# Order of the products inside a weight slot: feed-forward slots by length, projection slots by half of the weights

## The chip, the cores and the metric

The kernel runs on one core of a Trainium2 chip. Time is the device time of one execution in microseconds (us), median over several executions; lower is better.

## The reference, cut to what matters

The input is one sequence of 256 tokens of width 1024, in f32. A first block of two layers comes first, each with a gated feed-forward of width 2816, a mixer and a second feed-forward; behind it come an "even" layer (stick-breaking attention and a state-space mixer) and an "odd" layer (gated linear attention).

```
h = h + 0.5 * swiglu(rmsnorm(h, ffn1_norm[l]), gate, up, down)      # (silu(x@gate) * (x@up)) @ down
z = rmsnorm(h, mix_norm[l]) @ w_in[l]                               # 5664 columns, split over three branches
h = h + merged @ w_out[l]
h = h + 0.5 * swiglu(rmsnorm(h, ffn2_norm[l]), ...)
...                                                                 # even layer, odd layer: rms_norm(x) @ w_in, mix, @ w_out
```

Most of the arithmetic is products of a 256-row activation with f32 weight matrices, some 260 MB of them in all.

## The kernel before, in words

**Exact products from halves.** TensorE takes 32-bit operands in the type fp32r, which keeps fewer bits than f32. So each operand is split: high = value rounded to fp32r, low = value minus high. A product is high*high + high*low + low*high, all added up in PSUM. `exact3` issues those three as matmuls of 256 columns. For the feed-forward (`wide`, and the down products in `FfnApart.tensor`) the high and the low half of the activation lie side by side, so that one matmul of 512 columns does w_high*(x_high, x_low), and one of 256 columns does w_low*x_high. A reduction on VectorE (`take_wide`) adds the two halves of the bank when it is read.

**Slots.** Weights come in slots of 128 x 2048 (1 MB). Three buffers form a ring. Of each slot n SyncE issues the DMA into `w_raw` (`load`), ScalarE rounds it to `w_high` (`split_high`, L194, counts semaphore hi_made), VectorE subtracts for `w_low` (`split_low`, L201, counts lo_made), and TensorE uses both. `load` of slot n waits for lo_made of slot n-3; `split_high` of slot n waits until TensorE is through with slot n-3 (semaphore bank_filled). Each engine's order is written out by hand in the methods `scalar`, `vector` and `tensor` of each stage.

**What a slot is on TensorE.** A `wide` slot has 8 tiles k of 128 input channels and two groups i of 128 output features: 16 pairs of a 512-column and a 256-column product (L264 and L266), taking turns. There are 88 such slots, 22 in each of four feed-forwards. A down slot of `FfnApart` has 8 tiles, again 16 pairs (L725, L727); there are 33. A `project` slot has 8 tiles, two groups and three products of 256 columns each (L211, L212, L213), 48 products. There are 76: 22 in each of the two mixers, 20 in the even layer, 12 in the odd layer. Other slots (attention latents, branch and output matrices, the down slots of the last feed-forward) call `exact3` by themselves.

**Waits inside a slot.** At the start of a slot TensorE waits for lo_made. The first slot behind a norm also waits, at k = 0, 2, 4 and 6, for the low half of the activation `x` of these two tiles (`norm.x_low`, written at L302 on VectorE; the tiles 6 and 7 come from the last quarter of the stage before: TensorE fills the bank, VectorE reduces it (L242) and adds it to the residual (L691), ScalarE rounds it (L291), VectorE subtracts (L302)). The very first slot of the kernel comes in five pieces (FIRST_TILES: tiles 0; 1; 2, 3; 4, 5; 6, 7), each with its own waits. The argument `midway` calls a few small products in the middle of a slot: the norm's mean (L325, in the first feed-forward L366), latent sums, or transposes. Behind the mean come a square root on ScalarE (L334), a reciprocal on VectorE (L339) and the scaling of what was read from PSUM (L669, L675). VectorE reads a gate slot's banks at L242; the next gate slot waits for that read.

Of the kernel before, what the change touches and what calls it, by code (L numbers as in the profile page):

```python
# [15 lines left out]
P = 128  # L16
SEQ = 256
# [197 lines left out]

def project(c, pe, bank, n, kt, norm=None, tokens=False, width=FC, x=None, midway=None):

    wh, wl = c.weights_at(n, kt, width)
    xh, xl = x or (c.xh, c.xl)
    pe.wait_ge(c.lo_made, c.made(n))  # L220
    for k in range(kt):
        if midway and k == kt // 2:
            midway()
        if norm and k % 2 == 0:
            pe.wait_ge(*norm.x_low(k // 2 + 1))
        for i in range(2):
            start = k == 0 and i == 0
            if tokens:
                t = slice(i * P, (i + 1) * P)
                mm = exact3(pe, c.halves(bank)[:, i, 0:width], xh[:, k, t], xl[:, k, t], wh[:, k, :], wl[:, k, :],  # L230
                            start, k == kt - 1)
            else:
                f = slice(i * P, (i + 1) * P)
                mm = exact3(pe, c.halves(bank)[:, i, :], wh[:, k, f], wl[:, k, f], xh[:, k, :], xl[:, k, :],
                            start, k == kt - 1)
    return mm


# [6 lines left out]
def wide(c, pe, bank, n, norm=None, midway=None):  # L245


    wh, wl = c.weights_at(n, DT, FC)
    if n > 1:
        pe.wait_ge(c.lo_made, c.made(n))  # L250
    for k in range(DT):
        if midway and k == DT // 2:
            midway()
        if norm and n and k % 2 == 0:
            pe.wait_ge(*norm.x_low(k // 2 + 1))
        for b, (first, _) in enumerate(FIRST_TILES if n == 0 else ()):
            if k == first:
                pe.wait_ge(c.xl_made, b + 1)
                pe.wait_ge(c.lo_made, b + 1)
        if n == 1 and k % 4 == 0:  # L260
            pe.wait_ge(c.lo_made, PIECES + 1 + k // 4)
        for i in range(2):
            f = slice(i * P, (i + 1) * P)
            pe.matmul(c.bank(bank + i).rearrange("p (a t) -> p a t", a=2), wh[:, k, f], c.x[:, :, k, :], start=(k == 0),  # L264
                      stop=False, skip_group_check=True)
            mm = pe.matmul(c.bank(bank + i, SEQ), wl[:, k, f], c.xh[:, k, :], start=False, stop=(k == DT - 1),  # L266
                           skip_group_check=True)
    return mm


# [338 lines left out]
class FfnApart(Ffn):  # L609
# [90 lines left out]
    def tensor(self, pe):  # L700
# [12 lines left out]
        for m in range(FF_STEPS):  # L713
            n = base + 2 * FF_STEPS + m
            wh, wl = c.weights_at(n, SLOT_TILES, FC)
            pe.wait_ge(c.lo_made, c.made(n))
            for j in range(SLOT_TILES):
                p, k = divmod(SLOT_TILES * m + j, FF_TILES)
                if p == 0 and k % 2 == 0:
                    pe.wait_ge(*self.hid_low(k // 2 + 1))  # L720
                if p >= 2 and k == 0:
                    pe.wait_ge(*self.down_read(p - 1))
                for i in range(2):
                    f, bank = slice(i * P, (i + 1) * P), B_DOWN + 2 * (p % 2) + i
                    pe.matmul(c.bank(bank).rearrange("p (a t) -> p a t", a=2), wh[:, j, f], b.hid[:, :, k, :], start=(k == 0),  # L725
                              stop=False, skip_group_check=True)
                    mm = pe.matmul(c.bank(bank, SEQ), wl[:, j, f], b.hid[:, 0, k, :], start=False, stop=(k == FF_TILES - 1),  # L727
                                   skip_group_check=True)
                if k == FF_TILES - 1 and m < LAST:
                    mm.then_inc(c.done, 1)  # L730
            mm.then_inc(c.done, 1)

# [2343 lines left out]
```

## Time and profile before

| what | value |
|---|---|
| time, median of 3 runs | 1510.16 us (1507.58 to 1510.79) |
| the profiled execution's own time | 1510.64 us |
| its span | 1508.8 us |
| TensorE (PE) busy | 1499.7 us, 99%, 10908 matmuls |
| weight loads (PEld) busy | 1388.6 us, 92% |
| VectorE (DVE) busy | 1182.3 us, 78% |
| ScalarE (ACT) busy | 792.6 us, 53% |
| mean granted TensorE clock | 0.998 |
| DMA | 261.30 MB, 173 GB/s |

The span runs from the first to the last instruction; 1.8 us of the execution's time lie around it. A matmul in the trace has a start and a modelled end; matmuls overlap, so the "busy" time of one (0.28 us for 256 columns, 0.39 us for 512) is more than the distance to the next. How fast TensorE goes is read from start to start.

### The profile page before, as it was taken

How to read it: one execution, taken by the hardware profiler on the slowest of the kernel's cores; microseconds unless marked ns; L12 is line 12 of the kernel's file. 1: busy time of each engine (PE TensorE's matmuls, PEld its weight loads, DVE VectorE, ACT ScalarE, POOL GpSimd, SP SyncE). 2: the span in 40 equal slices, each digit the busy share in tenths (PEclk: the TensorE clock that was granted, in tenths of full speed). 3: DMA queues.
4: the chain of work that ended last, by engine and by line, in shares of the span. 5: the costliest groups of instructions: out<-in, count | busy, mean ns of one | idle time of the engine just before them, and what ended most of it. 6: DMA issues, size and time to landing. Idle time of an engine off the chain costs nothing.

```text
span 1508.8 us, 25562 instructions
## 1 busy us (share of the span) xinstructions
PE 1499.7 (99%) x10908; PEld 1388.6 (92%) x10908; DVE 1182.3 (78%) x1560; ACT 792.6 (53%) x1003; POOL 39.4 (3%) x41
## 2 busy tenths in 40 slices
PE   8999999999999999999999999999999999999999
PEld 7888899999988888888889999999999999999989
DVE  7987776797888865988758688889998899766744
ACT  6444455565544443544445556455545745775654
POOL 0000001210000000000001020000000000000000
PEclk9999999999999999999999999999999999999999
DMA  7555545434555545555554444465554453325531
GB/s 283 196 196 195 175 167 184 153 140 150 186 185 187 190 173 200 191 180 185 191 191 149 174 151 157 143 227 194 197 194 172 164 193 131 125 106 189 182 126 56
DMA packets 38976, 261.30 MB, mean 173 GB/s; under 512 B 4688, under 2 KB 5584, under 8 KB 9168
## 3 DMA queue, kind: packets, MB, share of 16 engines
q1 hardware_dynamic: 38000, 258.62, 47.8%
q8 instruction: 86, 1.41, 0.4%
q10 hardware_dynamic: 864, 1.05, 0.2%
q14 instruction: 26, 0.21, 0.0%
HBM read 258.61 MB, written 1.05 MB: 172 GB/s over the span
## 4 chain that ended last, share of the span: by engine, by line
PE 94%; DVE 4%; ACT 1%; DMA 0%; issue 0%; ACTq 0%
PE ps L264 22%; PE ps L211 14%; PE ps L213 14%; PE ps L212 14%; PE ps L266 11%; PE ps L725 8%; PE ps L727 4%; DVE w_low L201 2%; PE ps L1448 1%; DMA w_raw<-in_weights 0%; PE ps L1439 0%; PE ps L1421 0%; ACT w_high L194 0%; DVE scratch L2119 0%; PE ps L1463 0%; PE ps L2264 0%
## 5 line engine op out<-in xcount | busy, mean ns | idle before, releaser
L194 ACT ACTIVATE w_high<-w_raw 128x2048 fp32r<-128x2048 f32 (+2 forms) x244 | 459.8, 1886 | 423.2 <-PE ps L266 188.1
L201 DVE TENSOR_TENSOR w_low<-w_raw,w_high 128x2048 fp32r<-128x2048 f32 (+2 forms) x244 | 552.8, 2267 | 127.3 <-ACT w_high L194 125.3
L264 PE MATMUL ps<-x,w_high 128*128 128x512 f32 x1408 | 498.4, 399 | 2.5 <-DVE w_low L878 2.5
L266 PE MATMUL ps<-x,w_low 128*128 128x256 f32 x1408 | 394.8, 280 | 0.0
L264 PEld LDWEIGHTS ps<-x,w_high 128*128 128x128 f32 x1408 | 265.2, 188 | 67.2 <-DVE x L817 2.8
L266 PEld LDWEIGHTS ps<-x,w_low 128*128 128x128 f32 x1408 | 266.3, 189 | 0.1
L211 PE MATMUL ps<-x,w_high 128*128 128x256 f32 x904 | 261.0, 289 | 0.2 <-DVE x L302 0.2
L213 PE MATMUL ps<-x,w_low 128*128 128x256 f32 x904 | 255.7, 283 | 0.0
L212 PE MATMUL ps<-x,w_high 128*128 128x256 f32 x904 | 255.6, 283 | 0.0
L725 PE MATMUL ps<-ffn_hid,w_high 128*128 128x512 f32 x528 | 183.2, 390 | 0.0
L211 PEld LDWEIGHTS ps<-x,w_high 128*128 128x128 f32 x904 | 173.1, 192 | 5.1 <-issue 3.9
L212 PEld LDWEIGHTS ps<-x,w_high 128*128 128x128 f32 x904 | 173.3, 192 | 0.7 <-issue 0.5
L213 PEld LDWEIGHTS ps<-x,w_low 128*128 128x128 f32 x904 | 173.2, 192 | 0.0
L727 PE MATMUL ps<-ffn_hid,w_low 128*128 128x256 f32 x528 | 148.9, 282 | 0.0
L725 PEld LDWEIGHTS ps<-ffn_hid,w_high 128*128 128x128 f32 x528 | 99.1, 188 | 20.8
L727 PEld LDWEIGHTS ps<-ffn_hid,w_low 128*128 128x128 f32 x528 | 99.8, 189 | 0.0
L211 PE MATMUL ps<-w_high,x 128*128 128x256 f32 x320 | 92.3, 289 | 0.0
L213 PE MATMUL ps<-w_high,x 128*128 128x256 f32 x320 | 90.5, 283 | 0.0
L212 PE MATMUL ps<-w_low,x 128*128 128x256 f32 x320 | 90.5, 283 | 0.0
L242 DVE TENSOR_REDUCE ffn_up<-ps 128x512 f32<-128x1024 f32 x44 | 53.8, 1223 | 35.7 <-PE ps L266 35.5
L242 DVE TENSOR_REDUCE ffn_gate<-ps 128x512 f32<-128x1024 f32 x56 | 68.5, 1222 | 10.8 <-PE ps L266 5.1
L211 PE MATMUL ps<-mix_y_high,w_high 128*128 128x256 f32 x224 | 63.6, 284 | 0.0
(456 smaller groups left out, 2359.4 us busy)
## 6 DMA issues: line engine op xcount, KB each, us to landing
w_raw<-in_weights SPq DMA_DIRECT2D x231, 1024.0 KB, 4.8
w_raw<-in_weights SPq DMA_DIRECT2D x10, 768.0 KB, 4.2
w_raw<-in_weights SPq DMA_DIRECT2D x5, 512.0 KB, 3.8
even_second_vectors<-in_second SPq DMA_DIRECT2D x1, 1836.0 KB, 7.2
resid<-in_x SPq DMA_DIRECT2D x3, 256.0 KB, 6.5
w_raw<-in_weights ACTq DMA_DIRECT2D x3, 256.0 KB, 8.0
out<-resid SPq DMA_DIRECT2D x3, 256.0 KB, 2.4
table<-in_table SPq DMA_DIRECT2D x1, 737.0 KB, 8.3
```

Source lines behind the costliest of these rows:

```text
L194: act.activation(self.wh[:, j, 0:SIZES[n]], self.raw[:, j, 0:SIZES[n]], ACT.Copy).then_inc(self.hi_made, 1)
L201: dve.tensor_tensor(self.wl[:, j, 0:SIZES[n]], self.raw[:, j, 0:SIZES[n]], self.wh[:, j, 0:SIZES[n]].bitcast(F32), ALU.subtract).then_inc( ...
L211: pe.matmul(out, ah, bh, start=start, stop=False, skip_group_check=True)
L212: pe.matmul(out, ah, bl, start=False, stop=False, skip_group_check=True)
L213: return pe.matmul(out, al, bh, start=False, stop=stop, skip_group_check=True)
L242: return dve.tensor_reduce(out, c.ps[:, bank:bank + 2, :].rearrange("p f (a t) -> p f t a", a=2), AX.X, ALU.add)
L264: pe.matmul(c.bank(bank + i).rearrange("p (a t) -> p a t", a=2), wh[:, k, f], c.x[:, :, k, :], start=(k == 0), stop=False, skip_group_chec ...
L266: mm = pe.matmul(c.bank(bank + i, SEQ), wl[:, k, f], c.xh[:, k, :], start=False, stop=(k == DT - 1), skip_group_check=True)
L725: pe.matmul(c.bank(bank).rearrange("p (a t) -> p a t", a=2), wh[:, j, f], b.hid[:, :, k, :], start=(k == 0), stop=False, skip_group_check= ...
L727: mm = pe.matmul(c.bank(bank, SEQ), wl[:, j, f], b.hid[:, 0, k, :], start=False, stop=(k == FF_TILES - 1), skip_group_check=True)
L1448: mm = pe.transpose(c.bank(B_T)[:, i * P:(i + 1) * P], m.pr[:, 0, i * P:(i + 1) * P], ident)
```

## The change

In a `wide` slot and in a down slot of `FfnApart` all 512-column products come first and then all 256-column ones. In a down slot that holds the end of one pair of output groups and the start of the next, this is done for each pair by itself. In a `project` slot the products w_high*x_high and w_high*x_low of all tiles come first, then all w_low*x_high. TensorE waits for hi_made ahead of the first part and for lo_made ahead of the second. `midway` is called in the second part of a `wide` slot (still at k = 4), and at k = 6 instead of k = 4 in the first part of a `project` slot. Number, shape and operands of the products are the same, and so are the waits for `x_low`, at the same k. `exact3` and its other callers stay as they are.

```diff
--- before.py
+++ after.py
@@ -215,24 +215,30 @@
 
 def project(c, pe, bank, n, kt, norm=None, tokens=False, width=FC, x=None, midway=None):
 
+
     wh, wl = c.weights_at(n, kt, width)
     xh, xl = x or (c.xh, c.xl)
-    pe.wait_ge(c.lo_made, c.made(n))
+    pe.wait_ge(c.hi_made, c.made(n))
+
+    def product(k, i, w, moved, start=False, stop=False):
+        if tokens:
+            return pe.matmul(c.halves(bank)[:, i, 0:width], moved[:, k, i * P:(i + 1) * P], w[:, k, :], start=start, stop=stop,
+                             skip_group_check=True)
+        return pe.matmul(c.halves(bank)[:, i, :], w[:, k, i * P:(i + 1) * P], moved[:, k, :], start=start, stop=stop,
+                         skip_group_check=True)
+
     for k in range(kt):
-        if midway and k == kt // 2:
+        if midway and k == 3 * kt // 4:
             midway()
         if norm and k % 2 == 0:
             pe.wait_ge(*norm.x_low(k // 2 + 1))
         for i in range(2):
-            start = k == 0 and i == 0
-            if tokens:
-                t = slice(i * P, (i + 1) * P)
-                mm = exact3(pe, c.halves(bank)[:, i, 0:width], xh[:, k, t], xl[:, k, t], wh[:, k, :], wl[:, k, :],
-                            start, k == kt - 1)
-            else:
-                f = slice(i * P, (i + 1) * P)
-                mm = exact3(pe, c.halves(bank)[:, i, :], wh[:, k, f], wl[:, k, f], xh[:, k, :], xl[:, k, :],
-                            start, k == kt - 1)
+            product(k, i, wh, xh, start=k == 0 and i == 0)
+            product(k, i, wh, xl)
+    pe.wait_ge(c.lo_made, c.made(n))
+    for k in range(kt):
+        for i in range(2):
+            mm = product(k, i, wl, xh, stop=k == kt - 1)
     return mm
 
 
@@ -246,25 +252,33 @@
 
 
     wh, wl = c.weights_at(n, DT, FC)
-    if n > 1:
-        pe.wait_ge(c.lo_made, c.made(n))
-    for k in range(DT):
-        if midway and k == DT // 2:
-            midway()
-        if norm and n and k % 2 == 0:
-            pe.wait_ge(*norm.x_low(k // 2 + 1))
+    both = [(k, i, slice(i * P, (i + 1) * P)) for k in range(DT) for i in range(2)]
+
+    def arrived(parts, k):
+        if n > 1 and k == 0:
+            pe.wait_ge(parts, c.made(n))
         for b, (first, _) in enumerate(FIRST_TILES if n == 0 else ()):
             if k == first:
-                pe.wait_ge(c.xl_made, b + 1)
-                pe.wait_ge(c.lo_made, b + 1)
+                pe.wait_ge(parts, b + 1)
         if n == 1 and k % 4 == 0:
-            pe.wait_ge(c.lo_made, PIECES + 1 + k // 4)
-        for i in range(2):
-            f = slice(i * P, (i + 1) * P)
-            pe.matmul(c.bank(bank + i).rearrange("p (a t) -> p a t", a=2), wh[:, k, f], c.x[:, :, k, :], start=(k == 0),
-                      stop=False, skip_group_check=True)
-            mm = pe.matmul(c.bank(bank + i, SEQ), wl[:, k, f], c.xh[:, k, :], start=False, stop=(k == DT - 1),
-                           skip_group_check=True)
+            pe.wait_ge(parts, PIECES + 1 + k // 4)
+
+    for k, i, f in both:
+        if i == 0:
+            if norm and n and k % 2 == 0:
+                pe.wait_ge(*norm.x_low(k // 2 + 1))
+            for b, (first, _) in enumerate(FIRST_TILES if n == 0 else ()):
+                if k == first:
+                    pe.wait_ge(c.xl_made, b + 1)
+            arrived(c.hi_made, k)
+        pe.matmul(c.bank(bank + i).rearrange("p (a t) -> p a t", a=2), wh[:, k, f], c.x[:, :, k, :], start=(k == 0), stop=False,
+                  skip_group_check=True)
+    for k, i, f in both:
+        if i == 0:
+            if midway and k == DT // 2:
+                midway()
+            arrived(c.lo_made, k)
+        mm = pe.matmul(c.bank(bank + i, SEQ), wl[:, k, f], c.xh[:, k, :], start=False, stop=(k == DT - 1), skip_group_check=True)
     return mm
 
 
@@ -713,20 +727,23 @@
         for m in range(FF_STEPS):
             n = base + 2 * FF_STEPS + m
             wh, wl = c.weights_at(n, SLOT_TILES, FC)
-            pe.wait_ge(c.lo_made, c.made(n))
-            for j in range(SLOT_TILES):
-                p, k = divmod(SLOT_TILES * m + j, FF_TILES)
-                if p == 0 and k % 2 == 0:
-                    pe.wait_ge(*self.hid_low(k // 2 + 1))
-                if p >= 2 and k == 0:
-                    pe.wait_ge(*self.down_read(p - 1))
-                for i in range(2):
-                    f, bank = slice(i * P, (i + 1) * P), B_DOWN + 2 * (p % 2) + i
-                    pe.matmul(c.bank(bank).rearrange("p (a t) -> p a t", a=2), wh[:, j, f], b.hid[:, :, k, :], start=(k == 0),
+            pe.wait_ge(c.hi_made, c.made(n))
+            tiles = [(j, *divmod(SLOT_TILES * m + j, FF_TILES)) for j in range(SLOT_TILES)]
+            for pair in sorted({p for _, p, _ in tiles}):
+                own = [(j, k, i, slice(i * P, (i + 1) * P)) for j, p, k in tiles if p == pair for i in range(2)]
+                first = B_DOWN + 2 * (pair % 2)
+                for j, k, i, f in own:
+                    if pair == 0 and i == 0 and k % 2 == 0:
+                        pe.wait_ge(*self.hid_low(k // 2 + 1))
+                    if pair >= 2 and i == 0 and k == 0:
+                        pe.wait_ge(*self.down_read(pair - 1))
+                    pe.matmul(c.bank(first + i).rearrange("p (a t) -> p a t", a=2), wh[:, j, f], b.hid[:, :, k, :], start=(k == 0),
                               stop=False, skip_group_check=True)
-                    mm = pe.matmul(c.bank(bank, SEQ), wl[:, j, f], b.hid[:, 0, k, :], start=False, stop=(k == FF_TILES - 1),
-                                   skip_group_check=True)
-                if k == FF_TILES - 1 and m < LAST:
+                pe.wait_ge(c.lo_made, c.made(n))
+                for j, k, i, f in own:
+                    mm = pe.matmul(c.bank(first + i, SEQ), wl[:, j, f], b.hid[:, 0, k, :], start=False,
+                                   stop=(k == FF_TILES - 1), skip_group_check=True)
+                if own[-1][1] == FF_TILES - 1 and m < LAST:
                     mm.then_inc(c.done, 1)
             mm.then_inc(c.done, 1)
```

## Rows read from the trace of the kernel before

**Rows 1.** Waits of TensorE: who <- whom: us in total, times, longest.

```profile
PE ps L264 <- DVE w_low L878: 2.5, 1, 2.5
...
PE ps L2278 <- DVE scratch L2124: 1.0, 1, 1.0
```

**Rows 2.** Timeline, PE: start us, us, instruction; first products of `wide` and down slots.

```profile
36.08 0.39 PE L264 MATMUL ps<-x,w_high 128*128 128x512 f32 x1
...
130.37 0.39 PE L264 MATMUL ps<-x,w_high 128*128 128x512 f32 x1
...
141.48 0.39 PE L725 MATMUL ps<-ffn_hid,w_high 128*128 128x512 f32 x1
...
191.40 0.39 PE L725 MATMUL ps<-ffn_hid,w_high 128*128 128x512 f32 x1
...
434.45 0.40 PE L264 MATMUL ps<-x,w_high 128*128 128x512 f32 x1
...
536.21 0.40 PE L264 MATMUL ps<-x,w_high 128*128 128x512 f32 x1
```

**Rows 3.** Timeline, PE: six 512-column products in a row, and what follows.

```profile
228.25 0.39 PE L211 MATMUL ps<-w_high,mix_y_high 128*128 128x512 f32 x1
...
229.63 0.28 PE L211 MATMUL ps<-x,w_high 128*128 128x256 f32 x1
```

**Rows 4.** Timeline, PE: runs of 256-column products, first and last start.

```profile
1413.75 0.28 PE L211 MATMUL ps<-x,w_high 128*128 128x256 f32 x1
...
1425.27 0.28 PE L211 MATMUL ps<-w_high,x 128*128 128x256 f32 x1
...
1482.80 0.28 PE L211 MATMUL ps<-odd_o_high,w_high 128*128 128x256 f32 x1
...
1499.70 0.28 PE L211 MATMUL ps<-odd_o_high,w_high 128*128 128x256 f32 x1
```

**Rows 5.** Timeline, PE and DVE: start of slots behind a norm, and x_low.

```profile
196.95 0.28 PE L211 MATMUL ps<-x,w_high 128*128 128x256 f32 x1
...
200.07 0.88 DVE L302 SCALAR_TENSOR_TENSOR x<-resid,vectors,x 128x256 fp32r<-128x256 f32 x2 [0.98 <-ACT x L291]
...
417.06 0.39 PE L264 MATMUL ps<-x,w_high 128*128 128x512 f32 x1
...
418.93 0.88 DVE L302 SCALAR_TENSOR_TENSOR x<-resid,vectors,x 128x256 fp32r<-128x256 f32 x2 [0.98 <-ACT x L291]
...
602.87 0.39 PE L264 MATMUL ps<-x,w_high 128*128 128x512 f32 x1
...
606.00 0.88 DVE L302 SCALAR_TENSOR_TENSOR x<-resid,vectors,x 128x256 fp32r<-128x256 f32 x2 [0.98 <-ACT x L291]
```

**Rows 6.** Timeline, PE and DVE, of the kernel's first slot.

```profile
11.07 0.68 DVE L878 TENSOR_TENSOR w_low<-w_raw,w_high 128x512 fp32r<-128x512 f32 x1
11.67 0.87 DVE L817 SCALAR_TENSOR_TENSOR x<-resid,vectors,x 128x256 fp32r<-128x256 f32 x2
...
11.90 0.47 PE L264 MATMUL ps<-x,w_high 128*128 128x512 f32 x1 [2.51 <-DVE w_low L878]
...
15.29 0.63 PE L264 MATMUL ps<-x,w_high 128*128 128x512 f32 x1
15.71 0.41 PE L266 MATMUL ps<-x,w_low 128*128 128x256 f32 x1
...
17.71 0.39 PE L264 MATMUL ps<-x,w_high 128*128 128x512 f32 x1
```

**Rows 7.** Two stretches: busy us (instructions) of each engine, PEclk, DMA share, GB/s.

```profile
12.59:16.00 3.41, 3.41 (x13) 2.93 (x12) 3.02 (x5) 3.41 (x6) 0.00 (x0) 0.50 0.69 243
...
1252.00:1256.00 4.00, 2.98 (x28) 2.69 (x30) 3.90 (x10) 0.00 (x0) 0.00 (x0) 1.00 0.39 160
```

**Rows 8.** Timeline: the first norm's mean on PE, the second gate read on DVE.

```profile
26.03 1.89 PE L366 MATMUL ps<-scratch,ones 128*128 128x256 f32 x8
...
33.65 1.22 DVE L242 TENSOR_REDUCE ffn_gate<-ps 128x512 f32<-128x1024 f32 x1
```

## The prediction

> **What bounds the kernel now.** I read the page's busy times first: TensorE is busy for 99% of the span, VectorE for 78%, DMA moves 173 GB/s without anyone waiting long for it. The chain of waits says the same, since 94% of it is TensorE. The next view is the waits of TensorE, because the change gives it two waits where there was one: in the whole kernel it waits visibly for weights once, 2.5 us for the low half of a piece of the very first slot, and its only other wait of 1 us is for something else [rows 1]. So the later wait for lo_made has nearly nothing to take away. What is left is the distance from one product to the next, and this I read from starts.
>
> A `wide` slot runs at two speeds on the same tiles. From 36.08 to 130.37 are 17 slots: 94.29/17 = 5.546 us, 346.7 ns for a pair of a long and a short product. From 434.45 to 536.21 are 18 slots: 5.653 us, 353.3 ns for a pair. The down slots take 49.92/9 = 5.547 us, 346.7 ns a pair, from 141.48 to 191.40 [rows 2]. Going by the starts, 23 of the `wide` slots (368 pairs) run at the quick rate and 64 (1024 pairs) at the slow one; one is the first slot of the kernel. The streaming of the columns at the full clock of 2.4 GHz is 768/2.4 = 320 ns a pair, so there are 27 to 33 ns in a pair that are not columns. Only the order of products could change these.
>
> **Term 1, the distance between products.** No `wide` or down slot of the trace has its long products in a row. The nearest rows are six of 512 columns in the mixer: from 228.25 to 229.63, 1.38/6 = 230.0 ns each [rows 3]. Runs of 256 columns are plentiful. With `x` as an operand they take (1425.27-1413.75)/96 = 120.0 ns each, with another activation (1499.70-1482.80)/144 = 117.4 ns [rows 4]. I take 230.0 for every long product, 120.0 for a short one with `x` and 117.4 for a short one with the hidden activation. That gives a `wide` pair 350.0 ns and a down pair 347.4 ns. The sum is 368 x 3.3 ns = +1.2 us, 1024 x (-3.3 ns) = -3.4 us and 528 down pairs x 0.7 ns = +0.4 us, together -1.8 us.
>
> Both ends of this term: a long product at 226.7 ns (346.7 less 120.0, what the quick pairs leave for it) gives 0 for the quick `wide` pairs, 1024 x (-6.6) = -6.8 us for the slow ones and 528 x (-2.6) = -1.4 us for the down ones, -8.2 us in all. At 233.3 ns (353.3 less 120.0) it is +2.4, 0 and 528 x 4.0 = +2.1 us, +4.5 us in all. Six products are a thin base, so I keep both ends.
>
> The Trainium skill has a rule here. The page "TensorE: Matmul & The Clock Gate" gives, in the section "Back-to-back issue gap", N/2.4 + 2.5 ns from one product to the next at full clock, and its section "Step-by-step: what each phase is for" says that the next weights load beside the running product over a read port of their own. By that a pair would be 216 + 109 = 325 ns in any order, and this term would be 0 instead of -1.8 us. The trace disagrees on the size, 346.7 and 353.3 ns, and as one set of tiles shows both, something does depend on more than the number of columns.
>
> The 76 `project` slots keep 48 products of 256 columns with `x`, only in another order. Both roles of `x`, moving and stationary, sit at 120.0 ns in rows 4, and three sorts of neighbours take turns there, so I take 0. The other end is 117.4 ns for all 3648 products: -9.5 us. A loss I exclude up to a few tenths, since no long run of 256 columns in the trace is slower than 120.0.
>
> **Term 2, the x_low waits come earlier.** This is a cost. In the first slot behind a norm, the tiles k = 6 and 7 wait for their x_low. Today 36 products (`project`) or 12 pairs (`wide`) stand before this wait, some 4.2 us. Afterwards only 24 products of 120 ns (2.88 us) or 12 long products of 230 ns (2.76 us) do. The low products that could have filled the time are queued behind the waiting one.
> - First mixer: slot starts at 196.95, the wait is reached at 199.83, x_low is there at 200.07 + 0.88 = 200.95 [rows 5]. A release takes 0.15 us (w_low made at 11.75, product at 11.90 [rows 6]). Idle: 1.27 us. The second mixer starts in the same way: again 1.27 us.
> - Feed-forward behind a feed-forward: slot at 602.87, wait at 605.63, x_low at 606.88: 1.40 us [rows 5].
> - The two feed-forwards behind a mixer: slot at 417.06, wait at 419.82, x_low at 419.81 [rows 5]: 0.15 us each.
> The even layer's first slot gets its x_low from finer steps and the odd layer's is not changed: 0. Together 4.2 us. The chain up to x_low starts when TensorE fills the last bank of the stage before, so it doesn't come earlier by itself. Bounds: 0, if VectorE's chain were to shrink, and 5 us. An idle time of this length doesn't cost clock: around the wait at 1254 TensorE was idle 1.0 us and had 1.00 granted [rows 1, 7].
>
> **Term 3, the start.** Tiles 4 and 5 of the first slot have x_low at 11.67 + 0.87 = 12.54, so their long products start at about 12.65. The clock is at half (1.2 GHz) from 12.59 to 16.00 [rows 7], and a long product takes 15.71 - 15.29 = 0.42 us there [rows 6]. Eight of them end at about 16.05. Then all 16 short products are still to come, 16 x 0.12 = 1.9 us, and the slot ends at 17.95 instead of 17.71: +0.25 us.
>
> The mean of the first norm begins at 26.03, 2.77 us into its slot. In the new order it comes behind 16 long and 8 short products, 4.64 us, so 1.87 us later plus the 0.25: 28.15. From it depends everything up to the second gate read, which ends at 33.65 + 1.22 = 34.87 [rows 8] and would end at 36.98. The gate slot that waits for this read starts at 36.08 today [rows 2] and would be due at 36.08 + 0.25 + three slots at +0.05 = 36.5. Idle with the release: 0.6 us. Queued behind the later reciprocal on VectorE are the scaling, the next low half and this read; their own slack in weights is over two slots. In the later feed-forwards the mean has only 2 products and the same read has over 3 us of slack: 0. The `project` slots call `midway` behind 24 products before and after: 0. Term 3 is +0.9 us (0 to +2.4, if the clock came back later: then 16 short products at 0.21 us).
>
> **Waits for hi_made and lo_made**: one more wait for each slot. Slot boundaries have two or three waits now and show no gap in rows 2, so 0. ScalarE's and VectorE's releases (bank_filled at the end of a slot) don't move within it, and so the DMAs of SyncE stay where they are.
>
> **Sum:** -1.8 + 4.2 + 0.9 = +3.3 us on the profiled execution's 1510.64 us (span 1508.8 and 1.8 around it): 1513.9. That execution was 0.5 us above the median, 1510.16: forecast 1513.5 us.
>
> **The rivals.**
> A. The project slots leave the 120.0 ns rate and run at 117.4: +3.3 - 9.5 = -6.2 us, 1504.0. For it: other activations show this rate. Against: every slot with `x` settles at 120.0 whatever stands next to it.
> B. Long products in a row cost 226.7 ns: -8.2 + 4.2 + 0.9 = -3.1 us, 1507.1. For it: 226.7 and 120.0 are both the columns plus 13.3 ns. Against: rows 3. It decides for "faster" from about 229 ns downwards only if term 2 stays small.
> C. Long products in a row cost 233.3 ns: +4.5 + 5.1 = +9.6 us, 1519.8. For it: the slow pairs.
> D. The earlier waits cost nothing because something behind them, such as the 1.0 us at 1254, takes them up: -1.8 + 1 = about -1 us, 1509. Against: TensorE has no slack anywhere between 18 us and 1254 us to give back.
> E. The change doesn't do what it says, as no low half is waited for. This is not a case of its own; it is why no gain stands in the sum.
>
> **How the numbers follow.** Forecast 0.46, A 0.13, B 0.16, C 0.17, D 0.08. What a measurement of this kernel can tell from no change is 0.2%, 3.0 us. The forecast lies right at that border: 0.25 of it slower, 0.19 the same, 0.02 faster. A is faster, B half and half, C slower, D mostly the same. Faster 0.22, same 0.37, slower 0.41. The range leaves out about one in ten at each end: 1505 to 1519.5.
>
> **What would show it.** Right: in the three slots named above a wait of TensorE for x (DVE L302) of 1.2 to 1.4 us; a first down or `wide` slot of about 5.6 us everywhere, with 230 ns between long and 120 ns between short products; `project` slots unchanged at 5.76 us; the third gate slot at about 37.1 us. Wrong: `project` slots of 5.64 us (A), `wide` slots of 5.55 (B) or 5.65 us and more (C), no waits for x (D).

## The result, and the profile after

| | median | lowest to highest | executions |
|---|---|---|---|
| before | 1508.91 us | 1506.77 to 1512.09 | 20 |
| after | 1512.63 us | 1512.09 to 1513.83 | 20 |

The ratio is 1.0027, with a 95% interval of 1.002 to 1.0033: the change costs 3.7 us by the medians and 4.1 us (3.0 to 5.0) by the ratio, and 3.3 us were forecast. The profiled execution of the kernel after took 1512.38 us, at a mean granted clock of 1.0. Against the profiled execution of before (1510.64 us) that is only 1.7 us. The difference between 3.7 and 1.7 matters: after scatters by 1.7 us, before by 5.3 us, and its profiled execution was one of its longer ones. Experiment e5 bears on the reason.

The page after: the span, busy us (share) and instructions of each engine, the shares of the chain that ended last, and the costliest group.

```profile
span 1510.6 us, 25562 instructions
...
PE 1497.8 (99%) x10908; PEld 1388.9 (92%) x10908; DVE 1182.0 (78%) x1560; ACT 792.3 (52%) x1003; POOL 39.4 (3%) x41
...
PE 92%; DVE 5%; ACT 1%; DMA 1%; issue 0%; ACTq 0%
...
L274 PE MATMUL ps<-x,w_high 128*128 128x512 f32 x1408 | 337.9, 391 | 4.1 <-DVE x L834 2.5
```

Nothing here says "slower": same engine, same counts, busy time 1.9 us less. The busy time of a matmul whose end is modelled is no measure of this change. The waits and the starts are. The waits of TensorE after (who <- whom: us in total, times, longest), which answer to [rows 1]:

```profile
PE ps L274 <- DVE x L834: 2.5, 3, 0.9
PE ps L227 <- DVE x L316: 2.1, 2, 1.0
...
PE ps L274 <- DVE x L316: 1.2, 1, 1.2
PE ps L2295 <- DVE scratch L2141: 1.0, 1, 1.0
PE ps L274 <- DVE ffn_gate L248: 0.5, 1, 0.5
```

L316 writes x_low (L302 before), and L834 the x_low of the very first slot (L817 before). Three waits for it are new (two in `project`, L227, one in `wide`, L274), and one for the gate read. The weights' wait of 2.5 us in the very first slot has become a wait of 2.5 us for the first x_low.

The timeline of TensorE after (start us, us, instruction, idle before it and releaser): the second slot, the third gate slot, one `wide` slot, one down slot, the two sorts of new waits, and the stretch that was slow in [rows 2].

```profile
17.23 0.63 PE L274 MATMUL ps<-x,w_high 128*128 128x512 f32 x2
...
36.30 0.73 PE L274 MATMUL ps<-x,w_high 128*128 128x512 f32 x2 [0.49 <-DVE ffn_gate L248]
...
41.97 0.40 PE L274 MATMUL ps<-x,w_high 128*128 128x512 f32 x1
...
45.62 0.28 PE L281 MATMUL ps<-x,w_low 128*128 128x256 f32 x1
...
47.53 0.40 PE L274 MATMUL ps<-x,w_high 128*128 128x512 f32 x1
...
153.41 0.40 PE L740 MATMUL ps<-ffn_hid,w_high 128*128 128x512 f32 x1
...
157.14 0.28 PE L744 MATMUL ps<-ffn_hid,w_low 128*128 128x256 f32 x1
...
159.00 0.40 PE L740 MATMUL ps<-ffn_hid,w_high 128*128 128x512 f32 x1
...
202.27 0.39 PE L227 MATMUL ps<-x,w_high 128*128 128x256 f32 x1 [1.03 <-DVE x L316]
...
453.60 0.40 PE L274 MATMUL ps<-x,w_high 128*128 128x512 f32 x1
...
537.10 0.40 PE L274 MATMUL ps<-x,w_high 128*128 128x512 f32 x1
...
608.34 0.50 PE L274 MATMUL ps<-x,w_high 128*128 128x512 f32 x1 [1.16 <-DVE x L316]
```

From 453.60 to 537.10 are 15 `wide` slots: 83.50/15 = 5.567 us, where the slow slots of before took 5.653 and the quick ones 5.546. So a pair takes 347.9 ns. Its long products take (45.62-41.97)/16 = 228.1 ns, its short ones (47.53-45.62)/16 = 119.4 ns. In the down slot the long ones take (157.14-153.41)/16 = 233.1 ns and the short ones (159.00-157.14)/16 = 116.3 ns. This slot takes 5.59 us; the mean over the stage is 5.600, 0.053 more than in [rows 2].

The stretch of [rows 7] at the start, now (busy us of each engine, PEclk, DMA share, GB/s):

```profile
12.59:16.00 3.41, 2.47 (x14) 1.81 (x13) 2.25 (x5) 3.41 (x7) 0.00 (x0) 1.00 0.70 238
```

The clock is granted in full where before had half (0.50). That helps the first slot of this execution and is not an effect of the change, as e6 shows.

### The profile page after: what moved, and what is told of

Its sections match the earlier page's. It is cut to its first block, busy times and chain, and to the rows that moved or that the text cites. A ratio compares the mean times of both kernels' runs of the same rounds, so it can differ in the third digit from the quotient of the medians.

```text
span 1510.6 us, 25562 instructions
## 1 busy us (share of the span) xinstructions
PE 1497.8 (99%) x10908; PEld 1388.9 (92%) x10908; DVE 1182.0 (78%) x1560; ACT 792.3 (52%) x1003; POOL 39.4 (3%) x41
## 4 chain that ended last, share of the span: by engine, by line
PE 92%; DVE 5%; ACT 1%; DMA 1%; issue 0%; ACTq 0%
PE ps L274 21%; PE ps L227 18%; PE ps L281 11%; PE ps L740 8%; PE ps L225 7%; PE ps L211 5%; PE ps L213 5%; PE ps L212 5%; PE ps L744 4%; DVE w_low L201 2%; PE ps L1465 1%; DMA w_raw<-in_weights 1%; PE ps L1456 0%; PE ps L1438 0%; ACT w_high L194 0%
## 5 line engine op out<-in xcount | busy, mean ns | idle before, releaser
L274 PE MATMUL ps<-x,w_high 128*128 128x512 f32 x1408 | 337.9, 391 | 4.1 <-DVE x L834 2.5
L274 PEld LDWEIGHTS ps<-x,w_high 128*128 128x128 f32 x1408 | 258.2, 188 | 56.5 <-DVE x L834 3.8
L227 PE MATMUL ps<-x,w_high 128*128 128x256 f32 x1792 | 230.3, 286 | 2.1 <-DVE x L316 2.1
L227 PEld LDWEIGHTS ps<-x,w_high 128*128 128x128 f32 x1792 | 219.3, 191 | 7.8 <-issue 4.3
L281 PEld LDWEIGHTS ps<-x,w_low 128*128 128x128 f32 x1408 | 181.0, 191 | 7.1
L281 PE MATMUL ps<-x,w_low 128*128 128x256 f32 x1408 | 184.0, 283 | 0.0
L227 PE MATMUL ps<-x,w_low 128*128 128x256 f32 x896 | 116.6, 283 | 0.0
L227 PEld LDWEIGHTS ps<-x,w_low 128*128 128x128 f32 x896 | 111.5, 192 | 0.0
L225 PE MATMUL ps<-w_high,x 128*128 128x256 f32 x640 | 83.1, 286 | 0.0
L225 PEld LDWEIGHTS ps<-w_high,x 128*128 128x128 f32 x640 | 78.4, 191 | 0.8 <-issue 0.3
L744 PE MATMUL ps<-ffn_hid,w_low 128*128 128x256 f32 x528 | 68.4, 279 | 0.0
L211 PE MATMUL ps<-mix_y_high,w_high 128*128 128x256 f32 x224 | 63.6, 284 | 0.0
L212 PE MATMUL ps<-mix_y_low,w_high 128*128 128x256 f32 x224 | 63.3, 282 | 0.0
L213 PE MATMUL ps<-mix_y_high,w_low 128*128 128x256 f32 x224 | 63.2, 282 | 0.0
```

Of the source, the lines that this page charges most:

```text
L211: pe.matmul(out, ah, bh, start=start, stop=False, skip_group_check=True)
L212: pe.matmul(out, ah, bl, start=False, stop=False, skip_group_check=True)
L213: return pe.matmul(out, al, bh, start=False, stop=stop, skip_group_check=True)
L225: return pe.matmul(c.halves(bank)[:, i, 0:width], moved[:, k, i * P:(i + 1) * P], w[:, k, :], start=start, stop=stop, skip_group_check=True)
L227: return pe.matmul(c.halves(bank)[:, i, :], w[:, k, i * P:(i + 1) * P], moved[:, k, :], start=start, stop=stop, skip_group_check=True)
L744: mm = pe.matmul(c.bank(first + i, SEQ), wl[:, j, f], b.hid[:, 0, k, :], start=False, stop=(k == FF_TILES - 1), skip_group_check=True)
```

## The experiments

Times are medians. A ratio is to the kernel before on the same chip, whose median there was 1508.28 us (e1 to e4), 1508.34 (e7 to e9) and 1508.60 (e10 to e12). The ratios are formed round by round, so they differ a little from the quotient of the medians.

### Each part alone: e1, e2, e3

**e1_wide**: only `wide` is new. **e2_project**: only `project`. **e3_down**: only the down slots.

```diff
# e1_wide: wide() of the kernel after in the kernel before
+    for k, i, f in both:
+        ...
+            arrived(c.hi_made, k)
+        pe.matmul(... wh[:, k, f], c.x[:, :, k, :] ...)
+    for k, i, f in both:
+        ...
+        mm = pe.matmul(... wl[:, k, f], c.xh[:, k, :] ...)
# e2_project: project() of the kernel after in the kernel before
+            product(k, i, wh, xh, start=k == 0 and i == 0)
+            product(k, i, wh, xl)
+    pe.wait_ge(c.lo_made, c.made(n))
+            mm = product(k, i, wl, xh, stop=k == kt - 1)
# e3_down: FfnApart's down slots of the kernel after in the kernel before
+            for pair in sorted({p for _, p, _ in tiles}):
```

> Only the order inside the `wide` slots is the new one; project and down slots are those of the kernel before. Theory (three terms): every wide slot takes 3.654 + 1.912 = 5.567 us as in the changed kernel, so against the profiled execution of before 64 slow slots give -5.5 us and 22 quick ones cost +0.4; the x_low wait behind a feed-forward costs 1.4 us once and 0.1 us twice, the second gate read 0.5 us; together about 1507.5 us, and within 1 us from run to run. Rival: the rates belong to the whole instruction stream and not to the order inside a slot; then slow wide slots of 5.65 us are seen again and the time scatters as that of before does (1506.8 to 1512.1).

> Only the order inside the `project` slots is the new one. Theory: the x_low wait at the head of each mixer costs 1.3 us, twice, and nothing else changes (products stay at 120.0 ns): +2.6 us against before, 1511.5 us. Rival: the mixers' slots cost nothing, because the chain behind the norm is the same length and is caught up: within 0.5 us of before.

> Only the order inside the down slots of the first three feed-forwards is the new one. Theory: 33 slots go from 5.547 to 5.600 us: +1.75 us against before, 1510.7 us, with long products at 233.4 ns and short ones at 116.6 ns. Rival: the 233.4 ns come from the neighbouring wide slots' new order (the rate is carried over from the slot before); then the down slots stay at 5.547 us here and the time is that of before.

| | median | lowest to highest | ratio (95%) |
|---|---|---|---|
| e1_wide | 1508.29 | 1507.41 to 1510.06 | 1.0002 (0.9994 to 1.0011) |
| e2_project | 1511.92 | 1510.03 to 1513.78 | 1.0029 (1.0019 to 1.0039) |
| e3_down | 1510.29 | 1506.9 to 1512.27 | 1.0009 (0.9998 to 1.002) |

`wide` comes out even, where 1507.5 us were expected: its gain on slow slots pays for its waits. Behind the start, its `wide` slots in the first three feed-forwards take 5.57 us, but for those that wait or call `midway`, and no stretch of them runs at 5.65; so the rate does belong to the order inside a slot. It scatters by 2.7 us, not by 1 us, but the kernel before scattered by 6.6 us on the same chip. The waits of TensorE in e1_wide (L268 is the long product, L310 x_low, L242 the gate read):

```profile
PE ps L268 <- DVE x L310: 1.2, 1, 1.2
...
PE ps L268 <- DVE ffn_gate L242: 0.5, 1, 0.5
```

`project` is the part that costs most. Its two waits are there:

```profile
PE ps L227 <- DVE x L308: 2.1, 2, 1.0
```

They take 1323 and 1325 ns from the start of one product to the next, where 120 ns stood before: 2.4 us. The products stay at 119.8 ns. The medians differ by 3.6 us, the ratio says 4.4 (2.9 to 5.9). The trace holds less: its profiled execution took 1510.27 us, the second shortest of eight that reach to 1513.78. It can be set against that of e5_before_again, since each has two of its feed-forwards at 5.65 us a `wide` slot. From the start of the second slot to the end of the span it takes 1508.5 - 16.58 = 1491.9 us, the other 1507.0 - 18.04 = 1489.0 us. That is 2.9 us, of which the two waits are 2.4. What the medians have beyond it fits the two rates of the old `wide` order, which e5 is about, but was not traced. e3_down's slots are 5.60 us throughout, as the theory had them, and 33 x 0.053 = 1.7 us lies between the 1.4 us of its ratio and the 2.0 us of its medians; its interval alone would allow no change at all. The three ratios add up to +0.4%, 6 us, against +0.27%, 4.1 us, for the whole change; each is uncertain by some 0.1%, so the sum says no more.

### The waits for x_low: e4

**e4_norm_old**: the kernel after, with the old order in the slots behind a norm.

```diff
 def project(c, pe, bank, n, kt, norm=None, ...):
+    if norm:
+        return project_old(c, pe, bank, n, kt, norm, tokens, width, x, midway)
 def wide(c, pe, bank, n, norm=None, midway=None):
+    if norm and n:
+        return wide_old(c, pe, bank, n, norm, midway)
```

> The changed kernel, but a slot that waits for x_low (first slot behind a norm, project and wide) keeps the old order of products. Theory: the three waits of 1.3 to 1.5 us and the two of 0.1 us go: -4.2 us against the changed kernel's 1512.6, so 1508.4 us, with no wait for x left above 0.2 us behind the start. Rival: the idle time moves to the next late chain (the mean, the root, the reads of the banks), and less than 2 us come back: 1510.6 us or more.

1508.52 us, 1507.8 to 1510.3, ratio 1.0006 (0.9997 to 1.0015). Against the median of 1512.63 us of the kernel after, 4.1 us come back; the two ratios, 1.0027 and 1.0006, say 3.2 us, with 1.0 and 1.4 us of uncertainty. The two profiled executions, both with the clock in full from before the first product on, took 1512.38 and 1508.19 us, 4.2 us apart. The waits of TensorE in e4_norm_old:

```profile
PE ps L327 <- DVE x L887: 2.3, 3, 1.3
PE ps L941 <- POOL eps L915: 1.6, 1, 1.6
PE ps L2348 <- DVE scratch L2194: 1.0, 1, 1.0
PE ps L327 <- DVE ffn_gate L273: 0.5, 1, 0.5
PE ps L211 <- DVE x L369: 0.2, 1, 0.2
```

x_low is L369 here. The lines for it in `project` and `wide`, 3.3 us after the change, are gone; the 0.2 us that are left at L211 (`exact3`) were there in the kernel after too. The others stand. So the earlier waits cost what they show, and nothing later takes them up. Term 2 is shown; rival D falls.

### The kernel before once more: e5

**e5_before_again**: no edit.

> The kernel before, unchanged, profiled once more. Theory: which wide slots run at 5.547 and which at 5.65 us is settled anew in each execution, so another number than 64 slow ones is seen, and the time differs from the first profile's by 0.1 us for each slot. Rival: the same slots are slow again, and the scatter of the kernel before (1505 to 1512 us) comes from elsewhere.

1508.82 us for the one profiled execution, 1.8 us less than the one the prediction was made from. The starts in its second feed-forward, in the same program:

```profile
437.40 0.39 PE L264 MATMUL ps<-x,w_high 128*128 128x512 f32 x1
...
531.70 0.39 PE L264 MATMUL ps<-x,w_high 128*128 128x512 f32 x1
```

94.30/17 = 5.547 us a slot, where [rows 2] has 5.653 for the same slots of the same kernel. About 20 slots fewer run at the slow rate, and 20 x 0.106 = 2.1 us. So which of the two rates this feed-forward settles at is not a property of its tiles, and it can differ from one execution of a program to the next. It is not a free draw for every stage, though. Of the four traces with the old `wide` order and `x` in its old place (before, e5_before_again, e2_project, e3_down) all have the first feed-forward quick and the last slow; the second is quick in one of them, the third in two. What decides is not shown. It fits the scatter: e2_project and e3_down, with the old `wide` order, spread over 3.8 and 5.4 us, the grouped e1_wide, e4_norm_old and the kernel after over 2.7, 2.5 and 1.7. And it corrects the base of the prediction: "64 slow slots" held for one execution.

### The mean earlier: e6

**e6_mean_early**: the kernel after, with the mean called at k = 6 of the long part of a `wide` slot.

```diff
             arrived(c.hi_made, k)
+            if midway and k == 3 * DT // 4:
+                midway()
...
-            if midway and k == DT // 2:
-                midway()
```

> The changed kernel, but the mean (midway) of a wide slot is called ahead of k = 6 among the long products, 2.75 us into the slot as in the kernel before, instead of 4.6 us. Theory: the third gate slot's wait for the read of its banks (0.77 us from product to product at 36.3) goes, all else stays: 0.5 us less in the trace. Rival: the wait was another one (weights, or the chain of the up slot) and stays.

1512.57 us, one execution. TensorE's waits, the starts of its second and of its fifth slot, and the windows view of the first slot:

```profile
PE ps L276 <- DVE x L834: 2.5, 2, 1.6
PE ps L227 <- DVE x L316: 2.0, 2, 1.0
PE ps L276 <- DVE x L316: 1.2, 1, 1.2
```

```profile
18.04 0.40 PE L276 MATMUL ps<-x,w_high 128*128 128x512 f32 x1
...
36.48 0.40 PE L276 MATMUL ps<-x,w_high 128*128 128x512 f32 x1
```

```profile
12.60:16.00 3.40, 3.40 (x8) 2.52 (x9) 2.63 (x5) 3.40 (x7) 0.00 (x0) 0.50 0.64 235
```

The wait for ffn_gate is gone, as term 3 has it. The total is not lower, since the first slot of this execution had half the clock (0.50) and ended at 18.04 us, where that of the kernel after ended at 17.23. Behind it the two traces can be compared. From the second slot's start to the fifth's are 36.48 - 18.04 = 18.44 us here and 36.30 - 17.23 = 19.07 us in the kernel after, so the wait for the gate read costs 0.6 us. From there to the end of the span both take 1474.3 us (1510.8 - 36.48 and 1510.6 - 36.30).

The half clock in the first slot is in four of the fourteen traces: before, e5 (there from 12.00 to 15.41 us), e6 and e10. Their first product starts at 7.34 to 7.63 us. In the other ten it starts at 7.83 us or later, and the clock is full from there on through that stretch.

### Only what gains: e7

**e7_wide_kept**: the kernel before, with the new order only in `wide` slots that are neither the first nor behind a norm, the mean early.

```diff
+def wide(c, pe, bank, n, norm=None, midway=None):
+    if norm or n == 0:
+        return wide_old(c, pe, bank, n, norm, midway)
+    ...
+            arrived(c.hi_made, k)
+            if midway and k == 3 * DT // 4:
+                midway()
```

> The kernel before, with the new order only in wide slots that are neither the first of all nor the first behind a norm, and with the mean 2.75 us into its slot. Theory: all wide slots at 5.567 us, nothing lost at waits, down slots at 5.547 us: against the wide-only kernel (1508.3) 1.5 us for x_low, 0.2 for the other two and 0.5 for the mean come back: 1506.1 us, steadier than before, 0.14% under it. Rival: the slots keep the old order's rates in part, or the gain is lost in the scatter of before: 1508 us.

1505.77 us, 1504.56 to 1508.12, ratio 0.9983 (0.9975 to 0.9992). All waits for x_low and for the gate read are back at before's size, and the `wide` slots keep 5.57 us: this half of the change by itself gains 2.6 us (1.2 to 3.8).

### Two long, two short: e8

**e8_two_two**: the kernel before; in `wide` the two long products of a tile, then its two short ones.

```diff
         for i in range(2):
             f = slice(i * P, (i + 1) * P)
             pe.matmul(... wh[:, k, f], c.x[:, :, k, :] ...)
+        for i in range(2):
+            f = slice(i * P, (i + 1) * P)
             mm = pe.matmul(... wl[:, k, f], c.xh[:, k, :] ...)
```

> The kernel before, with the wide slots' products in twos: both long ones of a tile k, then both short ones. If every change between long and short costs (grouped slots lose 20 ns a slot against 16 x 346.7 ns, in the products next to a change), eight times as many changes give slots of 5.7 us, +0.13 us x 88 over the quick rate, some 1515 us. If instead the rate is one that the pattern of lengths settles into, the slots have one fixed time between 5.547 and 5.65 us and the total is between 1504 and 1511 us with little scatter.

1505.22 us, 1504.61 to 1506.47, ratio 0.998 (0.9971 to 0.9989). If each change between lengths cost something, this order, with 16 changes a slot, would be far dearer than the grouped one with 1. It is as good. Its timeline:

```profile
53.20 0.62 PE L264 MATMUL ps<-x,w_high 128*128 128x512 f32 x2
53.66 0.40 PE L268 MATMUL ps<-x,w_low 128*128 128x256 f32 x2
53.89 0.63 PE L264 MATMUL ps<-x,w_high 128*128 128x512 f32 x2
54.36 0.39 PE L268 MATMUL ps<-x,w_low 128*128 128x256 f32 x2
```

From 53.20 to 53.89 and on to 54.36 the starts repeat: two pairs take 0.69 us, a slot 5.57 to 5.59 us. "Changes of length cost" falls. What both orders do is to keep out of the pattern in which long and short take turns one by one, the only one for which I saw the 353.3 ns. The time was forecast to lie between 1504 and 1511 us with little scatter, and it does, within 1.9 us.

### Operands at another address: e9, e11

That 256-column products take 120.0 ns with `x` and 117.4 ns with another activation [rows 4] made me ask whether it is the place of `x` in SBUF. **e9_shift** and **e11_shift64** are the kernel before with an unused tile ahead of `x`, declared with 48 and 64 bytes in each partition; all tiles behind it move too.

```diff
         self.h = sb("resid", [P, DT, SEQ])
+        self.apart = sb("apart", [P, 12])     # e9_shift; [P, 16] in e11_shift64
         self.x = sb("x", [P, 2, DT, SEQ], F32R)
```

> The kernel before, with an unused tile of 12 numbers (48 bytes) a partition placed ahead of x in SBUF, so that x and all tiles behind it lie 48 bytes further on; no instruction differs. Theory: where the operands lie against one another decides between 120.0 and 117.4 ns for a short product, x being the only activation at a round address: products with x leave 120.0 ns, and 76 project slots get up to 0.12 us shorter each, -9 us, 1500 us. Rival: the address is of no importance (the order of the three products, the engine beside it decide) and all slots keep their times.

> The kernel before with 64 unused bytes ahead of x instead of 48. If the address within 64 bytes is what counts, all rates are those of before (120.0 ns with x) and so is the time, 1508.3 us. If any move of the tiles counts, products with x leave 120.0 ns as with 48 bytes.

e9_shift: 1504.68 us, 1500.31 to 1509.64, ratio 0.9983 (0.9972 to 0.9995). e11_shift64: 1502.64 us, 1501.5 to 1503.71, ratio 0.9958 (0.9943 to 0.9972). The first and the last start of a run of 256-column products with `x`, in e9_shift (with one from the middle) and then in e11_shift64:

```profile
1399.24 0.28 PE L213 MATMUL ps<-x,w_high 128*128 128x256 f32 x1
...
1410.55 0.28 PE L213 MATMUL ps<-w_low,x 128*128 128x256 f32 x1
...
1421.20 0.28 PE L214 MATMUL ps<-w_high,x 128*128 128x256 f32 x1
```

```profile
1401.57 0.28 PE L213 MATMUL ps<-x,w_high 128*128 128x256 f32 x1
...
1423.54 0.28 PE L214 MATMUL ps<-w_high,x 128*128 128x256 f32 x1
```

They are 190 products apart: 21.96/190 and 21.97/190 = 115.6 ns each, against 120.0 in [rows 4]. But no product goes at 115.6 ns. Up to 1410.55 are 96 products, 11.31/96 = 117.8 ns, and behind it 94, 10.65/94 = 113.3 ns. In this run the rate changes where `x` changes its role in the product; in the mixers of the same trace both roles show both rates. The down slots became slower, 5.60 us. So the place of the operands in memory moves the rate of the same products by up to 6%, and again two rates stand side by side.

What e11_shift64 tests is not what I meant it to. In the built programs every tile starts at a multiple of 32 bytes, so a tile of 48 bytes takes up 64, and one of 16 takes up 32. How far the tiles lie from their place in the kernel before (there `x` starts at byte 98432 of each partition), with the times of this and the next section:

| | before | e9, e11 | e10 | e12 |
|---|---|---|---|---|
| `w_high`, `w_low` | 0 | 0 | 0 | 0 |
| `x` | 0 | +64 | +64 | +32 |
| every tile behind `x`, such as the hidden activation | 0 | +64 | +96 | +96 |
| short product with `x`, ns | 120.0 | 117.8, 113.3 | 117.8, 113.3 | 116.7, 118.3 |
| down slot (order of before), us | 5.547 | 5.600 | 5.617 | 5.618 |

e9_shift and e11_shift64 are the same program, instruction for instruction and address for address. Their medians, 1504.68 (ten executions) and 1502.64 (four), from two chips, lie 2.0 us apart all the same, and their first feed-forward ran at 5.58 us a `wide` slot in one trace and at 5.65 in the other; that is how far two small samples of one program can lie apart. The theory that what counts is the address within 64 bytes falls with both of them, for `x` moved by exactly 64 bytes and left 120.0 ns.

Of the 1500 us that were expected of e9_shift only its profiled execution came near, 1500.31 us, the shortest of the ten; the medians gain 3.7 us and not 9. Part of the rest goes with the clock: the five executions with a mean granted clock of 0.998 or less took 1505.1 to 1509.6 us, the five with 0.999 or 1.0 took 1500.3 to 1504.3.

### Both together: e10, e12

**e10_kept_shift** and **e12_kept_shift16**: e7_wide_kept with an unused tile ahead of `x` and one behind it, declared with 48 and 16 bytes, or 16 and 48. By this the tiles behind `x` were meant to move by 64 bytes in both; they move by 96.

```diff
+        self.apart = sb("apart", [P, 12])     # [P, 4] in e12_kept_shift16
         self.x = sb("x", [P, 2, DT, SEQ], F32R)
+        self.apart_too = sb("apart_too", [P, 4])     # [P, 12] in e12_kept_shift16
```

> The kernel with the new order in the later wide slots only (1505.8 us), with 48 unused bytes ahead of x and 16 behind it, so that only x moves off its address. Theory: project slots get to 117.4 ns and less for a product as in the first shifted kernel, down slots keep 5.547 us (they had 5.60 there, where the hidden activation had moved too): 8 us less in TensorE's work, of which VectorE's chain around 1250 takes 1 us: 1499 us. Rival: the quick rates need more than x moved, and 1503 to 1505 us are all.

> As the kernel with 48 bytes ahead of x and 16 behind, with 16 ahead and 48 behind. If every address off the 64-byte grid is as good, the time is the same, about 1499 us; if the distance counts, the rate of products with x is another one between 113 and 120 ns.

e10_kept_shift: 1496.51 us, 1493.47 to 1499.78, ratio 0.9915 (0.9898 to 0.9931). It is the fastest of all versions, 12 us under the kernel before and 16 us under the kernel after. Its `wide` slots take 5.49 and 5.54 us in turns, its short products with `x` 117.8 or 113.3 ns. Its down slots take 5.61 to 5.62 us and not the 5.547 that I expected from moving the tiles behind `x` by a whole 64 bytes; they lie 96 bytes on, but e9_shift, where it was 64, had 5.60 too. e12_kept_shift16: 1502.62 us, 1501.73 to 1506.24, ratio 0.9965 (0.9952 to 0.9977), with `wide` 5.60 and short products at 116.7 or 118.3 ns. So it is not enough that `x` lies off its old place: 32 bytes and 64 bytes give different rates, and different times. Which property of the address decides stays open; a sweep over it was not made.

In e10_kept_shift a part of the gain is lost again. The windows view before, during and after a stretch in the even layer:

```profile
1240.00:1243.85 3.85, 2.01 (x18) 1.83 (x17) 3.75 (x10) 0.00 (x0) 0.00 (x0) 1.00 0.52 217
```

```profile
1244.70:1251.40 6.70, 6.70 (x57) 6.09 (x50) 5.26 (x9) 5.09 (x12) 0.00 (x0) 0.50 0.44 157
```

```profile
1251.50:1255.00 3.50, 3.50 (x33) 3.50 (x31) 3.36 (x8) 0.00 (x0) 0.00 (x0) 1.00 0.00 0
```

TensorE comes earlier and waits 1.8 us for `scratch` instead of 1.0, and then has half the clock for 6.8 us. The other executions bear it out. Of the six of e10_kept_shift two have a mean granted clock of 1.0 and took 1493.5 and 1494.4 us; the four with 0.995 to 0.998 took 1496.2 to 1499.8. In e12_kept_shift16 four with 1.0 took 1501.7 to 1502.6 us, three with 0.997 took 1505.1 to 1506.2. So a stretch at half clock costs these versions about 3 us where it comes.

## Why the prediction was right, step by step

**Term 2, the x_low waits: right, and shown.** 4.2 us were forecast and e4_norm_old brings 4.1 back. From the start of one product to the next the three waits take 1309, 1301 and 1548 ns. Less the product itself that is 1.19, 1.18 and 1.32 us idle, where 1.27, 1.27 and 1.40 were worked out. The two slots behind a mixer lose 0.1 to 0.2 us each. The 4.1 us are from medians on two chips; the traces, 4.2 us apart, bear them out.

**Term 1, the distance between products: sign and order right, single sizes off.** Three of them:
- A `wide` pair takes 347.9 ns, not 350.0: long products with `x` settle at 227 ns (rival B's figure; 228.1 is the mean of a slot), and not at the 230.0 of the six in [rows 3]. The six were too few: in each slot of the kernel after, the first five or six starts lie 228 to 236 ns apart and only then 226 to 227.
- A down pair takes 350.0 ns, not 347.4: long products with the hidden activation settle at 233 (rival C's figure), short ones at 116.6. Taking one price for long products with either activation was the mistake, as [rows 4] already showed two prices for short ones.
- 64 slow slots were taken as the kernel's own. By e5_before_again they held for one execution only.

Against the profiled execution of before this term is 64 x (-0.086) + 23 x 0.021 + 33 x 0.053 = -3.3 us, where -1.8 was forecast. Against its median, which is 1.7 us less, it is -1.6 us; if all of that difference lies in slow slots, there are some 16 of them fewer (1.7/0.106, an estimate). That -1.6 comes so near to -1.8 is luck: the grouped `wide` slots came out 2.8 us better than forecast, the down slots 1.4 us worse and the base 1.7 us lower, and the errors cancel.

**Project slots: right.** 119.8 to 120.0 ns in the new order; rival A falls.

**Term 3, the start: mechanism and size right for the gate read, size not told for the first slot.** The third gate slot waits for the gate read, and e6_mean_early removes that wait and is 0.6 us shorter there. It stands at 36.30 us instead of the forecast 37.1, because the first slot had the full clock and ended at 17.23 instead of 17.71. The idle time there is 0.65 us, start to start less the product; 0.6 was forecast. For the first slot 0.25 us were forecast under half the clock. The kernel after had the full clock there. e6_mean_early, whose first slot is the same, had half: it started at 7.63 us as before did and ended at 18.04 instead of 17.71, 0.33 us later. But e5_before_again, with the old order, ended at 18.04 too.

**The waits for hi_made and lo_made: right.** None shows in the list behind the first slot.

**The sum.** -1.6 + 4.2, and 0.6 to 0.9 for the start, make 3.2 to 3.5 us, and +3.7 was measured. For the profiled executions the start makes 0.2 us (0.65 for the gate read, 0.48 back because the first slot ended at 17.23 instead of 17.71), so they give -3.3 + 4.2 + 0.2 = +1.1 against +1.7. About half a microsecond has no name. Rivals A and D are refuted; B and C each held for one of the two activations, which is why neither came about as a whole. E fell too: there is something to gain, 2.6 us in e7_wide_kept, though not from w_low, which nobody had waited for.

## What to carry to other kernels

When operands that arrive late are used first and the work that could wait with them is moved behind, count the work left ahead of each wait: here 1.4 us less of it in each of three places cost nearly 4 us, on an engine without slack. Take the same kernel's trace more than once before building on a rate that has two values in it, since a stage can run at the other one next time. Where an engine is busy for 99% of the span and yet 8% above its columns, try the placing of its operands beside the order of its instructions: moving `x` by 64 bytes and the tiles behind it by 96 took e7_wide_kept from 1505.8 to 1496.5 us, more than this whole change. Read the addresses off the built program when you do, for a tile may take up more than its size.

## What the runs showed of the hardware that I had not expected

- **A product costs more than its columns, and how much more depends on the operands and on where they lie.** At full clock 256 columns take 113.3 to 120.0 ns, and 512 columns 227 or 233 ns. Columns alone at 2.4 GHz are 106.7 and 213.3. With `x` in its old place both lengths cost 13.3 ns more than that (120.0 and 226.7), with the hidden activation the short ones 10 and the long ones 20 (116.6 and 233). The Trainium skill, page "TensorE: Matmul & The Clock Gate", section "Back-to-back issue gap", gives some 131 ns for 512 columns in a stream of weight loads and matmuls, and 216 ns for an isolated one; these measurements, for 32-bit operands, agree with neither. The Trainium skill's page "SBUF — State Buffer", section "SBUF: two separate sides", says that TensorE never waits on anyone at its ports; no run here shows whether another engine's reads have a part in these rates. What makes them depend on the place stays open.
- **Long and short in turns have two rates, 346.7 and 353.3 ns a pair**, one for a whole stage, and in the second feed-forward the one or the other in two executions of the same program. With `x` 64 bytes further on they are 348.9 and 353.3 ns (5.582 and 5.653 us a slot). Grouped (347.9) or two and two (348.3), only one rate was seen with `x` in its old place.
- **Half the clock behind a short wait.** In e10_kept_shift 6.8 us at 1.2 GHz followed a wait of 1.8 us, in a place where 1.0 us of idle time left the clock at 1.00 [rows 7]. Length alone doesn't decide it: in e9_shift the same wait was 1.8 us as well (1250.04 - 1248.21), and the windows view of it shows the clock at 1.00 throughout:

```profile
1248.00:1252.00 4.00, 2.17 (x46) 1.68 (x47) 3.93 (x7) 1.43 (x6) 0.00 (x0) 1.00 0.04 14
1252.00:1256.00 4.00, 4.00 (x42) 3.88 (x39) 3.93 (x9) 3.97 (x7) 0.00 (x0) 1.00 0.54 178
```

The prediction had claimed no cost for waits of 1.3 us, and this held.
